# A decoder step on one core: block gate by 128-column groups, sample tables loaded earlier, a re-planned instruction order

## The chip, the cores and the metric

One Trainium2 chip, one core of it. The metric is the device time of one execution in microseconds (us), lower is better. The core has TensorE (PE in the profile), VectorE (DVE), ScalarE (ACT), GpSimd (POOL) and SyncE (SP, which here only issues DMAs); "q" behind an engine's name is its sequencer, which issues DMAs and loads registers in the engine's own order.

## The reference

One layer of a decoder, for 512 prompt positions and for 8 samples (one new token each, 4096 past positions in a paged cache). What matters for the change is the samples' attention:

```python
k_full = cache_k[page_table[:, :own_first]].reshape(Bd, n_full, MOBA_BLOCK, H, D)   # 16 blocks of 256
kmean = jnp.mean(k_full, axis=2)
gate = jnp.einsum('bhtd,bnhd->bhtn', qf, kmean)          # 8 heads x 16 blocks per sample
_, sel = lax.top_k(gate, topk)                            # 3 blocks for each head
...
kg = cache_k[pages, :, hidx]; vg = cache_v[pages, :, hidx]
s = jnp.einsum('bhtd,bhtkd->bhtk', qf, kg) * scale        # scores with the chosen blocks, ALiBi, softmax
```

Besides that: RMSNorm, one input projection 1024 x 3584 (for prompt and samples), a gated MLP over chunks, the prompt's attention, and one output projection 1024 x 1024 with a norm and the residual. All of it is fp32.

## The kernel before

The prompt's projections run on PE as seven chunks of 512 columns (order k, q, v, u, va, ga, gb), each of 4 tiles (`pj(c, t)`), a tile in four quarters of two matmuls. The trace shows a fp32 matmul as two records, so a quarter is 4 records `PA<-...`. The weights of a chunk (2 MB, `wbuf`, two buffers) are loaded by SP (step `wl(c)`, line 825), which first waits until the chunk two before is multiplied and a given batch of keys has landed. `spj(c)` (line 1044, `SB<-wbuf,hTs`) is the same chunk for the 8 samples: for each of 8 slices of the contraction, four matmuls of 128 columns, each into its own 32 output partitions. The output projection has two such chunks, 7 and 8 (`op`, line 1210, for the prompt; `fopa` and `fop`, line 1044, for the samples).

The samples are worked off one after the other, b = 0 to 7. For one b:

- POOL loads the 16 key blocks (`ld(b, n)`, line 931, 512 KB each) into 18 slots, at most 5 in flight; a slot comes free when the selected keys of the batch before are multiplied.
- DVE adds the two halves of each block (`ks(b, n)`, line 744) into one of 6 `ksum` tiles.
- PE adds over the positions (`gs`, line 1226): a matmul with a window of `win`, in which one column is ones, puts the block's sum on one row of bank `GB`. Four blocks go together, one to each 32 output partitions, 512 columns each.
- DVE's `ga(b)` multiplies `GB` by the query row `qb` (spread over all partitions), reduces to 4 values for each head, transposes, gathers with four copies into `g16`, and takes the top 3 (lines 1634 to 1658).
- DVE and POOL multiply the selected keys by q (`ex`, line 757); `pg` looks up pages and spreads the choice (`spread`, `selP`, lines 1664 to 1677); `bc`, `mt`, `mb` on PE and DVE (one bank `DC`) give scores, maximum and weights.
- The chosen value pages are fetched one at a time (`fetch(b, half, k, j)`, four DMAs each, line 728): two of three choices by SP, one by POOL. `pv0(b)` and `pv1(b)` on PE (line 1257) are the products with the values.

On SP, `qst` (line 833) stores the samples' queries to DRAM (`q_rows`) and `qb(b)` (line 841) spreads row b over the partitions. Behind `qb(0)` stands `load_sample_tables()`: 20 small DMAs (gain, two bias tables, the post-norm gain, x of the samples) that are first read by `spj` of chunk va.

Every engine works its list strictly in order. The lists come from `make_plan()`, a planner that runs ahead of the build: each step has a duration and what it needs, and at each point the step that can start first is taken (lanes break ties). The durations, the landing times of early loads, and the clocks at which engines start are numbers in the code.

## Time and profile before

| | |
|---|---|
| three runs | 415.79, 418.33, 429.66 us; median 418.33 |
| profiled execution | 421.29 us, of which the span of the profile is 419.5 us |
| PE busy | 390.1 us (93%) |
| POOL / DVE / ACT busy | 278.5 / 263.2 / 124.8 us |
| HBM traffic | 106.31 MB read, 4.29 MB written, 264 GB/s over the span |

The sum of a prediction is made against the 421.29 us of the profiled execution, and its difference is then taken from the median. Times in rows are microseconds from the span's start unless marked ns.

### The profile page before, as it was taken

Reading aid. Unit: us, or ns where it says so; the run is one execution under the profiler, and the core shown is the slowest. Engines: PE = TensorE matmul, PEld = TensorE weight load, DVE = VectorE, ACT = ScalarE, POOL = GpSimd, SP = SyncE. Lnnn points to the kernel's source line nnn. Section 1 sums busy time; section 2 is a strip of 40 time slices with the busy share of each in tenths; the row PEclk is TensorE's granted clock in tenths of the full one; section 3 lists DMA queues with packets and bytes.
Section 4 is the critical chain, followed back from the end, with each engine's and each line's share of the span. In section 5 each row is a group of like instructions: output and inputs, shape, how many; then the busy total and the mean of one; then the engine's idle time right before and its main releaser. Section 6 shows DMA issues by size and latency. Waiting matters only on the chain.

```text
span 419.5 us, 9227 instructions
## 1 busy us (share of the span) xinstructions
PE 390.1 (93%) x2790; PEld 183.9 (44%) x2790; DVE 263.2 (63%) x695; ACT 124.8 (30%) x279; POOL 278.5 (66%) x438
## 2 busy tenths in 40 slices
PE   7779996999999999999879999999898899989994
PEld 4534354334533454444534546345332454344451
DVE  1165495446944696459746996579656865694532
ACT  4211110000121436446634357546242012011020
POOL 6867764484668766757878777688768856675011
PEclk9999998999999999999989999999999899999998
DMA  8999389999599899977998199975999999925121
GB/s 274 368 395 375 123 268 381 336 287 284 198 352 361 189 354 345 333 185 270 292 316 241 34 367 344 308 155 155 337 367 328 318 380 397 198 63 108 67 99 53
DMA packets 78599, 111.22 MB, mean 265 GB/s; under 512 B 45744, under 2 KB 46896, under 8 KB 78552
## 3 DMA queue, kind: packets, MB, share of 16 engines
q0 software_dynamic: 22576, 71.45, 50.7%
q1 hardware_dynamic: 51992, 36.79, 31.3%
q10 hardware_dynamic: 3984, 2.41, 1.9%
q8 instruction: 22, 0.36, 0.4%
q14 instruction: 25, 0.20, 0.2%
HBM read 106.31 MB, written 4.29 MB: 264 GB/s over the span
## 4 chain that ended last, share of the span: by engine, by line
PE 18%; SPq 14%; DMA 7%; issue 7%; DVE 4%; POOL 3%; DVEq 1%; POOLq 0%; ACT 0%; ACTq 0%
PE PA L1210 14%; SPq L728 11%; DMA K<-in_cache_k,kidx 3%; DMA wbuf<-in_w_out 3%; DVE ksum L757 2%; DMA V<-in_cache_v 2%; POOL K L931 1%; SPq L724 1%; PE GB L1226 1%; PE SB L1044 1%; SPq L726 1%; PE SB L1196 1%; PE DC L1257 1%; POOL rstd L950 1%; POOL ksum L757 0%
## 5 line engine op out<-in xcount | busy, mean ns | idle before, releaser
L1101 PE MATMUL PA<-wbuf,hT 128*128 128x512 f32 x384 | 181.7, 611 | 1.2 <-DMA wbuf<-in_w_in 1.0
L931 POOL DMA_INDIRECT K<-in_cache_k,kidx x128 | 134.2, 1049 | 69.2 <-issue 36.4
L744 DVE TENSOR_TENSOR ksum<-K 128x512 f32<-128x512 f32 x128 | 86.2, 690 | 59.1 <-DMA K<-in_cache_k,kidx 52.6
L1101 PEld LDWEIGHTS PA<-wbuf,hT 128*128 128x128 f32 x384 | 69.2, 193 | 76.8 <-issue 74.2
L728 POOL DMA_DIRECT2D V<-in_cache_v x128 | 76.4, 599 | 16.8 <-issue 11.0
L1210 PE MATMUL PA<-wbuf,hT 128*128 128x512 f32 x128 | 59.2, 604 | 0.1
L757 DVE TENSOR_TENSOR ksum<-K,qb 128x128 f32<-128x128 f32 x128 | 41.1, 394 | 1.6 <-DVE selT L1658 1.3
L757 POOL TENSOR_TENSOR ksum<-K,qb 128x128 f32<-128x128 f32 x64 | 30.4, 507 | 12.2 <-DVE selT L1658 11.1
L1226 PE MATMUL GB<-ksum,win 128*32 128x512 f32 x256 | 34.1, 604 | 4.8 <-DVE ksum L744 4.8
L1210 PEld LDWEIGHTS PA<-wbuf,hT 128*128 128x128 f32 x128 | 22.9, 189 | 25.7 <-issue 25.2
L1101 PE MATMUL PA<-hT,wbuf 128*128 128x512 f32 x64 | 29.0, 599 | 0.0
L1690 DVE TENSOR_REDUCE sc<-ksum 128x48 f32<-128x3072 f32 x8 | 26.6, 3327 | 0.0
L1044 PE MATMUL SB<-wbuf,hTs 128*32 128x128 f32 x576 | 19.3, 289 | 6.3 <-DMA wbuf<-in_w_in 6.1
L1393 ACT ACTIVATE pr<-pr,smin 128x128 f32<-128x128 f32 (+3 forms) x32 | 17.7, 555 | 22.9 <-DVE smin L1580 22.8
L1359 ACT ACT_TABLE_LOAD x13 | 16.7, 1283 | 21.8 <-PE PA L1101 21.7
L947 POOL TENSOR_TENSOR rstd<-msum,nhalf 128x1 f32<-128x1 f32 x6 | 3.3, 550 | 27.6 <-DVE msum L1612 14.7
L1044 PEld LDWEIGHTS SB<-wbuf,hTs 128*32 128x32 f32 x576 | 16.4, 116 | 10.3 <-DMA wbuf<-in_w_in 5.0
L1402 ACT COPY pT<-SB 128x128 f32<-128x128 f32 (+3 forms) x32 | 12.6, 427 | 23.3 <-PE SB L1164 21.9
L1101 PEld LDWEIGHTS PA<-hT,wbuf 128*128 128x128 f32 x64 | 11.6, 190 | 13.7 <-issue 13.6
L1580 DVE CUSTOM_DVE_ANT_0 pr<-alibi,SB 128x128 f32<-128x128 f32 (+3 forms) x32 | 14.3, 484 | 4.4 <-PE SB L1155 4.3
L1257 PE MATMUL DC<-V,pex 128*32 128x64 f32 x768 | 13.9, 220 | 3.2 <-DMA V<-in_cache_v 3.2
L1305 ACT ACTIVATE junk<-PA 128x512 bf16<-128x512 f32 x8 | 4.8, 598 | 39.7 <-PE PA L1210 39.7
(226 smaller groups left out, 371.9 us busy)
## 6 DMA issues: line engine op xcount, KB each, us to landing
wbuf<-in_w_in SPq DMA_DIRECT2D x6, 2048.0 KB, 10.8
V<-in_cache_v SPq DMA_DIRECT2D x240, 32.0 KB
V<-in_cache_v POOLq DMA_DIRECT2D x128, 32.0 KB, 6.4
wbuf<-in_w_out SPq DMA_DIRECT2D x2, 2048.0 KB, 21.6
wbuf<-in_w_in SPq DMA_DIRECT2D x4, 512.0 KB, 10.3
K<-in_cache_k,kidx POOLq DMA_INDIRECT x128, 8.0
qb<-q_rows SPq DMA_DIRECT2D x8, 256.0 KB
v<-in_x_prompt ACTq DMA_DIRECT2D x2, 512.0 KB, 9.6
```

What stands on the lines that cost most here:

```text
L728: eng.dma_start(V[j * ROWS:(j + 1) * ROWS, x * TOP + k, :, :], v_pages[bass.ds(page, 1), :, :, HEAD[x] * HD:(HEAD[x] + 1) * HD] .rearrange ...
L744: eng.tensor_tensor(ksum[:, n % SUMS, :], K[:, at, 0, :], K[:, at, 1, :], ALU.add).then_inc(s_dsum, 1)
L757: last = eng.tensor_tensor(kq[:, x * TOP + k, :, :], K[:, bass.ds(n, 1), :, col:col + HD].rearrange("p a r d -> p (a r) d"), qb[:, col:col ...
L931: pool.indirect_dma_start(K[:, m % SLOTS, :, :].rearrange("p r w -> p (r w)"), None, k_rows, bass.IndirectOffsetOnAxis(ap=kidx[:, b, n:n + ...
L1044: last = pe.matmul(bank[32 * j:32 * j + 32, 0:P], src[:, kc, :], w[:, kc, j * P:(j + 1) * P], start=(kc == kcs[0]), stop=(kc == kcs[-1]), ...
L1101: last = pe.matmul(bank[:, :], lhs, rhs, start=(kc == 0), stop=(kc == KC - 1))
L1210: last = pe.matmul(bank[:, :], hT[:, kc, t * P:(t + 1) * P], wbuf[:, c % 2, kc, :], start=(kc == 0), stop=(kc == KC - 1))
L1226: last = pe.matmul(GB[32 * j:32 * j + 32, :], win[:, 31 - g:63 - g], ksum[:, (4 * g + j) % SUMS, :], start=(g == 0), stop=(g == G - 1), ti ...
L1257: last = pe.matmul(DC[32 * j:32 * j + 32, hh * HD:(hh + 1) * HD], pex[:, h, i, r:r + 1].broadcast_to([P, 32]), V[:, h * TOP + i, r, :], st ...
L1359: act.activation(dst, bank, fn, scale=sc_).then_inc(pa_free[n % 2], 1)
L1393: act.activation(pr[:, hh, 0:(i + 1) * P], pr[:, hh, 0:(i + 1) * P], ACT.Exp, bias=smin[:, hh:hh + 1], scale=-1.0, accum_out=ssum[:, 2 * p ...
L1690: dve.tensor_reduce(sc[:, :, :, :].rearrange("p h k r -> p (h k) r"), kq[:, :, :, :], AX.X, ALU.add).then_inc(s_scr, 1)
```

## The change

1. **Gate by 128-column groups.** The partition groups of the array now hold the four groups of 128 columns (two heads each) instead of four blocks: for each block there are four matmuls of 128 columns, group j reads `ksum[:, n, 128j:128j+128]`, and block n lands on row n of each partition group. The result is [4 x 32, 128] instead of [4 x 32, 512]. So `ga` multiplies 128 columns, reduces in four instructions of 32 partitions, and needs no gathering copies. `GB` holds two batches side by side (halves by b % 2), so `gs` of b no longer waits for `ga(b-1)` but for `ga(b-2)`. The blocks are summed in five lots, 4, 4, 4, 2, 2, instead of four of 4.
2. **A second spread of q.** `ga` needs q by groups of 128 columns: four more small DMAs in each `qb(b)`, ahead of the old one, into `qg` (the tile `qs`). `ga` waits on these (`s_qg`), and `multiply_selected` now waits for the old `qb` itself.
3. **Sample tables** are issued right behind the other small tables, ahead of everything in SP's list.
4. **Planner numbers**: a fetch on SP or ACT 4.2 instead of 3.1 us, values landed 4.0 instead of 2.5 us behind the last one, SP's start 28 instead of 20 us, `ga` 2.8 instead of 3.3, `qb(0)` 3.0 instead of 4.0, and the new `gs` steps. All engines' lists are made anew from them.

```diff
+BATCHES = [(0, 4), (4, 8), (8, 12), (12, 14), (14, 16)]
...
-            add("SP", "spread", ("qb", 0), 4.0, ("SP", ("qst",)))
+            add("SP", "spread", ("qb", 0), 3.0, ("SP", ("qst",)))
...
-                    add(eng, "fetch", ("fetch", b, hh, k, j), 2.5 if eng == "POOL" else 3.1, ("DVE", ("pg", b)), *free, *more)
+                    add(eng, "fetch", ("fetch", b, hh, k, j), 2.5 if eng == "POOL" else 4.2, ("DVE", ("pg", b)), *free, *more)
...
-        ends[eng, s] = clock[eng] + (0.0 if eng != "Q" else 2.5 if s[0] == "v" else 0.8)
+        ends[eng, s] = clock[eng] + (0.0 if eng != "Q" else 4.0 if s[0] == "v" else 0.8)
...
-PLAN_START = {"PE": 4.5, "ACT": 3.5, "DVE": 1.0, "POOL": 8.4, "SP": 20.0, "Q": 12.0}
+PLAN_START = {"PE": 4.5, "ACT": 3.5, "DVE": 1.0, "POOL": 8.4, "SP": 28.0, "Q": 12.0}
...
+            load_sample_tables()
             for s in PLAN["SP"]:
...
+                    sp.wait_ge(*((s_gate, b) if b else (s_snr, 1)))
+                    for j in range(G):
+                        sp.dma_start(qg[32 * j:32 * j + 32, :],
+                                     q_rows[b:b + 1, j * P:(j + 1) * P].broadcast_to([32, P])).then_inc(s_qg, 16)
                     sp.dma_start(qb[:, :], q_rows[b:b + 1, :].broadcast_to([P, W])).then_inc(s_qb, 16)
-                    if b == 0:
-                        load_sample_tables()
...
-                    if g == 0 and b >= 1:
-                        pe.wait_ge(s_gate, b)
-                    for j in range(4):
-                        last = pe.matmul(GB[32 * j:32 * j + 32, :], win[:, 31 - g:63 - g],
-                                         ksum[:, (4 * g + j) % SUMS, :], start=(g == 0), stop=(g == G - 1),
-                                         tile_position=(0, 32 * j))
+                    if g == 0 and b >= 2:
+                        pe.wait_ge(s_gate, b - 1)
+                    for n in range(lo, hi):
+                        for j in range(G):
+                            last = pe.matmul(GB[32 * j:32 * j + 32, (b % 2) * P:(b % 2 + 1) * P], win[:, 31 - n:63 - n],
+                                             ksum[:, n % SUMS, j * P:(j + 1) * P], start=(n == 0), stop=(n == NB - 1),
+                                             tile_position=(0, 32 * j))
...
-                    dve.wait_ge(s_qb, 16 * (b + 1))
-                    dve.tensor_tensor(sumq, GB[:, :], qb[:, :], ALU.mult).then_inc(s_gate, 1)
+                    dve.wait_ge(s_qg, 16 * G * (b + 1))
+                    dve.tensor_tensor(sumq, GB[:, (b % 2) * P:(b % 2 + 1) * P], qg, ALU.mult).then_inc(s_gate, 1)
...
-                    link(dve.tensor_reduce(g128[:, 0:H].rearrange("p (x j) -> p j x", x=2),
-                                           sumq.rearrange("p (j x d) -> p j x d", j=G, x=2), AX.X, ALU.add))
-                    link(dve.transpose(gT[:, :], g128[:, :]))
-                    for j in range(4):
-                        last = dve.tensor_copy(g16[:, :, j], gT[32 * j:32 * j + H, 0:G])
+                    for j in range(G):
+                        last = dve.tensor_reduce(g128[0:32, j:H:G], sumq[32 * j:32 * j + 32, :].rearrange("p (x d) -> p x d", x=2),
+                                                 AX.X, ALU.add)
                     link(last)
-                    gates = g16[:, :, :].rearrange("h g j -> h (g j)")
+                    link(dve.transpose(gT[0:32, :], g128[0:32, :]))
+                    gates = gT[0:H, 0:NB]
```

How SP's list stands near its beginning, before (from the last of the first small tables; `ks`, `yb` and `v` are stores of new rows):

```order
L789 DMA gain<-in_sgu_gain 128x512
L811 DMA out<-ks 8x128 x4
L807 DMA out<-yb 128x512
L833 DMA q_rows<-qs 8x128 x4
L841 DMA qb<-q_rows 128x512
L795 DMA gains<-in_sgu_gain 32x128
L796 DMA w<-in_sgu_w 32x1
L797 DMA b<-in_sgu_b 32x1
L798 DMA gposts<-in_g_post 32x2x128
L799 DMA xs<-in_x_sample 8x2x128
```

The last five rows come four times; then `out<-yb` twice and the weights of chunk 2. Now, from the last row of the tables' fourth round:

```order
L807 DMA xs<-in_x_sample 8x2x128
L820 DMA out<-ks 8x128 x4
L842 DMA q_rows<-qs 8x128 x4
L852 DMA qs<-q_rows 32x128 x4
L854 DMA qb<-q_rows 128x512
L816 DMA out<-yb 128x512 x3
L834 DMA wbuf<-in_w_in 128x8x512
```

So the 20 table DMAs moved from behind `qb` to ahead of `ks` and `q_rows`, and the weights of chunk 2 lost them from in front.

PE's list from the third lot of key sums of b = 0 (`GB`) to the first lot of b = 1, before (`spread` is `bc(0)`, `mx` is `mt(0)`, `SB<-wbuf,hTs` is `spj` of chunk 2):

```order
L1226 MATMUL GB<-ksum,win 32x512 x4
L1136 MATMUL SB<-ident,yb 128x128 x4
L1101 MATMUL PA<-wbuf,hT 128x512 x6
L1128 MATMUL SB<-pr,one 128x128 x4
L1101 MATMUL PA<-hT,wbuf 128x512 x2
L1136 MATMUL SB<-ident,yb 128x128 x4
L1101 MATMUL PA<-hT,wbuf 128x512 x6
L1233 MATMUL DC<-spread,one 128x24
L1101 MATMUL PA<-hT,wbuf 128x512 x2
L1044 MATMUL SB<-wbuf,hTs 32x128 x32
L1238 MATMUL DC<-ident,mx 8x128
L1101 MATMUL PA<-hT,wbuf 128x512 x2
```

and now (its first row is the last lot of b = 0):

```order
L1239 MATMUL GB<-ksum,win 32x128 x8
L1112 MATMUL PA<-wbuf,hT 128x512 x2
L1147 MATMUL SB<-ident,yb 128x128 x4
L1112 MATMUL PA<-wbuf,hT 128x512 x6
L1139 MATMUL SB<-pr,one 128x128 x4
L1112 MATMUL PA<-hT,wbuf 128x512 x2
L1147 MATMUL SB<-ident,yb 128x128 x4
L1112 MATMUL PA<-hT,wbuf 128x512 x4
L1246 MATMUL DC<-spread,one 128x24
L1112 MATMUL PA<-hT,wbuf 128x512 x4
L1251 MATMUL DC<-ident,mx 8x128
L1055 MATMUL SB<-wbuf,hTs 32x128 x32
```

The last key sums of b = 0 stand a quarter earlier, `bc(0)` a quarter earlier, and `mt(0)` now stands ahead of the samples' chunk 2.

PE's list near the end of the input projections, before (`SB<-wbuf,hTs` is `fopa(0)`, the first reader of the output weights; `SB<-ident,ya` turns the prompt's result):

```order
L1257 MATMUL DC<-V,pex 32x64 x24
L1101 MATMUL PA<-wbuf,hT 128x512 x4
L1251 MATMUL DC<-psm,one 32x2 x4
L1257 MATMUL DC<-V,pex 32x64 x24
L1101 MATMUL PA<-wbuf,hT 128x512 x2
L1196 MATMUL SB<-ident,ya 128x128 x4
L1044 MATMUL SB<-wbuf,hTs 32x128 x16
```

and now:

```order
L1270 MATMUL DC<-V,pex 32x64 x24
L1112 MATMUL PA<-wbuf,hT 128x512 x8
L1055 MATMUL SB<-wbuf,hTs 32x128 x16
L1112 MATMUL PA<-wbuf,hT 128x512 x6
L1264 MATMUL DC<-psm,one 32x2 x4
L1270 MATMUL DC<-V,pex 32x64 x24
L1239 MATMUL GB<-ksum,win 32x128 x16
L1207 MATMUL SB<-ident,ya 128x128 x4
```

The first reader of the output weights stands three quarters of a tile ahead of the end of the input projections, which it followed before; behind it come those quarters, the second value product of b = 5 and the first key sums of b = 7.

## Rows read from the trace of the kernel before

**Rows 1.** The page: busy time of each engine.
```profile
PE 390.1 (93%) x2790; PEld 183.9 (44%) x2790; DVE 263.2 (63%) x695; ACT 124.8 (30%) x279; POOL 278.5 (66%) x438
```

**Rows 2.** Who PE waited for: us in total, times, longest us.
```profile
PE SB L1044 <- DMA wbuf<-in_w_in: 6.1, 3, 3.5
PE GB L1226 <- DVE ksum L744: 4.8, 4, 1.7
PE DC L1257 <- DMA V<-in_cache_v: 3.2, 2, 2.5
PE DC L1055 <- DVE sc L1715: 2.1, 1, 2.1
PE DC L1251 <- issue: 2.0, 1, 2.0
```

**Rows 3.** SP's queue in order of time: start us, us, what.
```profile
17.98 13.18 SPq L789 DMA_DIRECT2D sgub<-in_sgu_b  x1
31.20 3.84 SPq L789 DMA_DIRECT2D gain<-in_sgu_gain  x1
35.09 1.38 SPq L811 DMA_DIRECT2D out<-ks  x4
...
36.92 1.35 SPq L833 DMA_DIRECT2D q_rows<-qs  x4
46.13 0.34 SPq L841 DMA_DIRECT2D qb<-q_rows  x1
...
56.46 0.67 SPq L799 DMA_DIRECT2D xs<-in_x_sample  x1
...
58.21 0.39 SPq L825 DMA_DIRECT2D wbuf<-in_w_in  x1
```

**Rows 4.** PE in order of time, first two batches; idle before it in brackets.
```profile
31.42 1.95 PE L1044 MATMUL SB<-wbuf,hTs 128*32 128x128 f32 x64
...
43.01 5.42 PE L1101 MATMUL PA<-wbuf,hT 128*128 128x512 f32 x12
...
69.08 3.43 PE L1044 MATMUL SB<-wbuf,hTs 128*32 128x128 f32 x64 [3.48 <-DMA wbuf<-in_w_in]
...
74.36 1.06 PE L1226 MATMUL GB<-ksum,win 128*32 128x512 f32 x8
```

**Rows 5.** DVE in order of time, around the gate of b = 0.
```profile
34.04 0.28 DVE L1548 TENSOR_TENSOR mix<-qs,ks 128x128 f32<-128x128 f32 x1
...
49.49 0.69 DVE L1634 TENSOR_TENSOR ksum<-GB,qb 128x512 f32<-128x512 f32 x1 [3.24 <-PE GB L1226]
...
51.18 0.89 DVE L1642 COPY g<-gT 8x4 f32<-8x4 f32 x4
...
60.00 0.17 DVE L1673 TENSOR_TENSOR spread<-ident,vals 8x24 f32<-8x24 f32 x1
...
66.38 0.20 DVE L1704 TENSOR_REDUCE mx<-sc 128x8 f32<-128x48 f32 x1
```

**Rows 6.** Line 728, value fetches: from issue to landing.
```profile
DMA to landing us min/median/max: 2.0/6.4/9.7
```

**Rows 7.** 45 to 50 us: busy PE, PEld, DVE, ACT, POOL; clock, DMA, GB/s.
```profile
45.00:50.00 5.00, 5.00 (x21) 1.97 (x21) 1.25 (x3) 0.69 (x1) 3.83 (x17) 1.00 0.20 63
```

**Rows 8.** PE in order of time, from 215 us on.
```profile
215.04 0.24 PE L1055 MATMUL DC<-msum,fold 128*32 128x1 f32 x8 [2.12 <-DVE sc L1715]
215.21 7.11 PE L1101 MATMUL PA<-wbuf,hT 128*128 128x512 f32 x12
...
301.51 1.07 PE L1226 MATMUL GB<-ksum,win 128*32 128x512 f32 x8 [1.71 <-DVE ksum L744]
...
326.71 0.88 PE L1257 MATMUL DC<-V,pex 128*32 128x64 f32 x48 [2.50 <-DMA V<-in_cache_v]
```

**Rows 9.** DVE: the last key block of b = 6.
```profile
317.05 0.69 DVE L744 TENSOR_TENSOR ksum<-K 128x512 f32<-128x512 f32 x1 [2.27 <-DMA K<-in_cache_k,kidx]
```

**Rows 10.** Line 825, weight loads: from issue to landing.
```profile
DMA to landing us min/median/max: 9.2/11.0/21.6
```

More of the change, by code:

```diff
@@ L53, in v_queue, with batch_of @@
     return ("SP", "POOL", "ACT")[k]
+def batch_of(n):
+    return [lo <= n < hi for lo, hi in BATCHES].index(True)
 def make_plan():
@@ L248, in make_plan @@
             if n >= SUMS:
-                deps.append(("PE", ("gs", b, (n - SUMS) // 4)))
+                deps.append(("PE", ("gs", b, batch_of(n - SUMS))))
             add("DVE", "gate", ("ks", b, n), 0.75, *deps)
@@ L252, in make_plan @@
             add("POOL", "load", ("const",), 8.5)
-        for g in range(G):
-            late = [("DVE", ("ks", b, n)) for n in range(4 * g, 4 * g + 4)]
-            add("PE", "gate", ("gs", b, g), 1.0, *late, *([("DVE", ("ga", b - 1))] if b else []))
+        for g, (lo, hi) in enumerate(BATCHES):
+            late = [("DVE", ("ks", b, n)) for n in range(lo, hi)]
+            add("PE", "gate", ("gs", b, g), 0.25 * (hi - lo), *late, *([("DVE", ("ga", b - 2))] if b >= 2 else []))
         used = [("Q", ("v", b - 2, hh, k)) for hh in range(2) for k in range(TOP)] if b >= 2 else []
-        add("DVE", "gate", ("ga", b), 3.3, ("PE", ("gs", b, G - 1)), ("SP", ("qb", b)), *used)
+        add("DVE", "gate", ("ga", b), 2.8, ("PE", ("gs", b, len(BATCHES) - 1)), ("SP", ("qb", b)), *used)
         parts = [("ex", b, i) for i in range(PARTS)]
@@ L506, in hymba_kernel @@
         iota16 = sb("iota16", [H, NB])
-        g16 = sb("g16", [H, G, 4])
         top8 = sb("top8", [H, 8])
@@ L602, in hymba_kernel @@
         s_qb = sem("q_row_spread")
+        s_qg = sem("q_row_spread_by_groups")
         s_yas = sem("yas_ready")
@@ L624, in hymba_kernel @@
         kq = ksum[:, :, :].rearrange("p s (x r d) -> p (s x) r d", x=4, r=2)
-        sumq = ksum[:, 0, :]
+        sumq = ksum[:, 0, 0:P]
+        qg = qs[:, :]
         xres = [qT[:, 0:2, :], qT[:, 2:4, :], kT[:, 0:2, :], kT[:, 2:4, :]]
@@ L741, in sum_rows @@
             if n >= SUMS:
-                eng.wait_ge(s_gs, G * b + (n - SUMS) // 4 + 1)
+                eng.wait_ge(s_gs, len(BATCHES) * b + batch_of(n - SUMS) + 1)
             at = (NB * b + n) % SLOTS
@@ L746, in multiply_selected @@
         def multiply_selected(eng, b, which, name):
+            eng.wait_ge(s_qb, 16 * (b + 1))
             rows = {}
@@ L1219, in _ @@
                     b, g = s[1], s[2]
-                    pe.wait_ge(s_dsum, NB * b + 4 * g + 4)
+                    lo, hi = BATCHES[g]
+                    pe.wait_ge(s_dsum, NB * b + hi)
                     if (b, g) == (0, 0):
                         pe.wait_ge(s_ones, 1)
-                    if g == 0 and b >= 1:
-                        pe.wait_ge(s_gate, b)
-                    for j in range(4):
-                        last = pe.matmul(GB[32 * j:32 * j + 32, :], win[:, 31 - g:63 - g],
-                                         ksum[:, (4 * g + j) % SUMS, :], start=(g == 0), stop=(g == G - 1),
-                                         tile_position=(0, 32 * j))
+                    if g == 0 and b >= 2:
[5 more added lines that the diff above has]
+                                             tile_position=(0, 32 * j))
                     last.then_inc(s_gs, 1)
@@ L1631, in _ @@
                     b = s[1]
-                    dve.wait_ge(s_gs, G * (b + 1))
-                    dve.wait_ge(s_qb, 16 * (b + 1))
-                    dve.tensor_tensor(sumq, GB[:, :], qb[:, :], ALU.mult).then_inc(s_gate, 1)
+                    dve.wait_ge(s_gs, len(BATCHES) * (b + 1))
+                    dve.wait_ge(s_qg, 16 * G * (b + 1))
+                    dve.tensor_tensor(sumq, GB[:, (b % 2) * P:(b % 2 + 1) * P], qg, ALU.mult).then_inc(s_gate, 1)
                     dve.wait_ge(s_gate, b + 1)
```

## The prediction

> **What bounds the kernel now.** I read the page first: PE is busy for 390.1 of 419.5 us [rows 1], so no other engine bounds the whole, and everything but PE's work and PE's waits is cover. What a change can win is the 29.4 us of idle, and of these only what lies between the start and the end. So the second view is the list of whom PE waited for [rows 2]: 6.1 us for input weights in three waits, 4.8 for key blocks, 3.2 for values, 2.1 for a score step on DVE that held bank `DC`, 2.0 for another value landing; 18.2 us in all. A wait also costs clock: behind the 3.48 us wait at 69.08 the 64 records of `spj` took 3.43 us, against 1.95 for the same 64 at 31.42 [rows 4], so 1.5 us; behind the wait at 215.04, 12 records took 7.11 us [rows 8] against 5.42 [rows 4], so 1.7 us. At 326.71 there is another wait of that size [rows 8], and I count 1.7 us there too. The third view is SP's queue [rows 3]: it tells why the first long wait is there.
>
> **Sample tables (SP).** Before, the 20 table DMAs run from 46.47 (the end of `qb(0)`) to 57.13 us: 10.7 us, 0.53 us each [rows 3]. The weights of chunk 2 are issued behind them, at 58.21, and PE stands until 69.08 [rows 3, 4]. In the change nothing but `qb(0)` and three stores is in front. The weights then wait for their own condition, PE's end of chunk 0: PE runs 12 records from 43.01 [rows 4], and with what the new list puts up to the end of chunk 0 that comes at 55 to 56 us. So they are issued some 3 us earlier, at a time at which the DMA engines are at 0.20 of their capacity [rows 7]. A load takes 9.2 to 21.6 us, median 11.0 [rows 10]; on quiet engines I take the low end, and they land at about 65, ahead of `spj`. The wait and its clock go.
>
> But every DMA that moves forward is moved past something. The tables are now ahead of `out<-ks` and of the store of q. The store, issued at 36.92 before, is issued after 35.04 + 10.7 + 1.4 = 47.1 and is through at 48.5. Before, SP waited from 38.27 to 46.13 for that store to land [rows 3], under key loads; now it falls where the engines are quiet [rows 7], and I take the shortest landing of a small DMA in the trace, 2.0 us [rows 6]: 50.5. Then four small spreads, 0.53 each, 52.6, and again 2.0: q is there for `ga(0)` at 54.6 us. Before, `ga(0)` began at 49.49, and what it waited for was PE, not q [rows 5]. So q takes the place of the weights as what is late: by about 5 us.
>
> How much of this reaches PE: `ga` gets shorter (next part) by 1.0 us, so from its start to `spread` it is 60.17 - 49.49 - 1.0 = 9.7 us, and from there to the end of `mx` 66.58 - 60.17 = 6.4, less 0.7 for the 512-column step of chunk q that stood between and now stands behind: 5.7 [rows 5]. `mt(0)` can start at q + 15.5. Behind it PE has 4.0 us (`mt`, `spj`, one quarter, and the semaphore between) to the first key sums of b = 1: q + 19.6, which is 74.2 us with q at 54.6. Before, it was 74.36 [rows 4]. Without the late q, PE would be there at 70.2: from 43.01 on 9 quarters of 1.8, 1.0 of key sums, 1.9 of small steps and `bc` to 62.3, two quarters, then 4.0 and some tenths. **Term 1: -4.2 for the weights, +4.0 for q, -0.2 us.** Ends: with q at 52 it is -2.7; with landings of 6.4 us instead of 2.0 [rows 6] only for the spreads it is +4.2.
>
> **Gate by groups.** PE: before, a lot of four blocks is 8 records in 1.0 to 1.1 us [rows 4]. After it is 32 records of 128 columns, in four partition groups. The same form is in the trace: `spj`, 64 records in 1.95 us [rows 4], so 32 in 0.98. The columns streamed are the same and so is the time. The extra lot of each batch splits a run of matmuls once more; a new run costs about 0.15 us (5.42 for 12 against 3 x 1.75), so 8 x 0.15 = **term 2: +1.2 us**. The bank is shared by two batches, which removes a wait of PE that is in no row; nothing.
>
> On this there is a rule of the Trainium skill that speaks against the change (page "TensorE: Matmul & The Clock Gate", section "Back-to-back issue gap"): in a stream of weight loads and matmuls the sustained spacing is about 81 ns at 128 columns and 131 ns at 512. By it, four short ones would cost 2.5 times one long one. The 8 x 16 x 2 = 256 records of the gate at some 0.13 us each are 34 us, and would become 84. The trace has 30 ns for a record of 128 columns in partition groups, so I don't follow the rule here.
>
> DVE: one multiplication of 0.69 becomes 0.28, the price of 128 columns [rows 5]; the reduction, as long, becomes four of 128 columns, which I price at the 0.28 of the multiplication; four copies, 0.89, go. 0.69 + 0.69 + 0.89 = 2.3 against 0.28 + 1.1 = 1.4: `ga` is 0.9 to 1.0 us shorter. DVE is busy 63% and bounds nothing; the gain lies on the chain from `ga` to the freeing of key slots, and shortens each batch's cycle of loads. Against it, SP issues four more spreads (2.1 us) between `ex` and the fetches of values, of which some 1 us falls into its wait for `selP`. For values the two cancel; for keys 1 us is left.
>
> **New order.** This is the part that can win, and it can't be priced step by step. What goes: the wait of 2.1 us at 215.04 with its 1.7 us of clock, because the step that needed bank `DC` there (`ra`, the samples' norm) now stands far behind. **Term 3: -3.8 us.** What may go: 4.8 for keys, 3.2 + 1.7 for values, 2.0 at the second product of b = 6 [rows 2, 8]. The list gives `bc` and the second value product of several batches 5 to 8 us of PE work more room. But it moves the key sums of b = 5 and 6 forward by 4 to 5 us of PE work, and there the keys were late already: PE waited 1.71 at 301.51, and the last block of b = 6 came 2.27 us late for DVE too [rows 8, 9]. The cycle of key loads is 1 to 1.5 us faster now, not 4 to 5. The first value product of b = 5 also stands nearer to its gate, by some 3 us, where it waited 2.50 [rows 8]. And `fopa(0)` is moved ahead of 5.4 us of projection, 0.9 of value product and 1.0 of key sums: the output weights have that much less time. I take it that in this part new waits are as large as those that go, 10.5 us against 10.5: **term 4: 0**, with ends -10 and +8.
>
> **Sum**: -0.2 + 1.2 - 3.8 + 0 = -2.8 us; 421.29 becomes 418.5. The median of the runs is 2.96 below the profiled one, so I forecast 418.33 - 2.8 = **415.5 us**, no difference that this kernel's measurement can tell (about 2%, 8.4 us).
>
> **Rivals.**
> - *All late waits vanish.* The new fetch durations fit the trace, and no wait replaces the old ones: -2.8 - 10.5 = -13.3 on the median, 405 us. For it: the fetches on SP really were longer than the plan had them. Against it: the key cycle [rows 9].
> - *The tables stall SP* (slower). The engines are full at 35 us; a small table was held 13.18 us in SP's queue at 17.98, and the next 3.84 [rows 3]. If the 20 DMAs take 1.0 us each instead of 0.53, q comes at 64 and PE at 83.6 instead of 74.2: +9.4, 425 us. It turns slower from q at 57.4 on. Against it: the nine DMAs issued from 35.09 to 38.27 were not held [rows 3].
> - *The output weights are late* (slower). If they take 21.6 us instead of 11.0 [rows 10] with the reader 7.3 us earlier, PE stands about 8 us more at `fopa(0)`, and there is nothing else in its list: 423.5 us. From a landing of some 3 us over the median on, it costs more than the other terms win.
> - *Short matmuls are not free.* Were each priced at even double its columns, the gate's 34 us would double: 452 us. The rows of `spj` exclude it nearly. The skill's spacing would give 466, and its chance is in here.
>
> **How the numbers follow.** Forecast 0.50; vanishing waits 0.20; stalled tables 0.12; late output weights 0.13; short matmuls 0.02; the rest, 0.03, is near no change. Faster by over 2% (under 410.0) needs most of the late waits gone: 0.20. Slower by over 2% (over 426.7) needs a rival at its upper end or two of them: 0.13. Within 2%: 0.67. The range reaches to the vanishing waits and to the stalled tables: 405 to 425.
>
> **What would show it.** Right: no wait at `spj` of chunk 2, waits of PE of about 2 us each at `bc(0)` and `mt(0)`, `ga(0)` starting at 54 to 55 us behind a DMA of `qs`, first key sums of b = 1 at 74 to 75; the wait at `ra` gone; 32 gate records in about 1 us; waits for keys near b = 6 still there. Wrong: `ga(0)` before 51 or after 58, a gate lot of 1.5 us or more, or the sum of PE's waits in the last third under 3 or over 15 us.

## The result: 4.4% slower

| | before | after |
| --- | --- | --- |
| median of 4 runs, us | 419.98 (415.79 to 429.66) | 438.96 (433.53 to 441.15) |
| ratio, 95% interval | 1 | 1.0443 (1.0274 to 1.0613) |
| profiled execution, us | 421.29 | 439.66 |
| its span, us | 419.5 | 437.7 |
| its mean granted clock of TensorE | 0.985 | 0.972 |

The changed kernel is 19 us slower, outside the range of 405 to 425. All ratios in this section leave disturbed runs out, so a ratio can differ a little from that of two medians.

The busy line of the page after the change, beside [rows 1]:

```profile
PE 398.2 (91%) x3558; PEld 206.2 (47%) x3558; DVE 258.3 (59%) x687; ACT 123.5 (28%) x278; POOL 278.3 (64%) x438
```

PE is busy 8.1 us longer and idle 39.5 us instead of 29.4; the two make the 18.2 us of the span. Only 3.6 of the 8.1 lie in the gate's records (37.7 us against 34.1). The granted clock tells of more. It has two levels, full and half, and its mean of 0.985 before and 0.972 after means about 13 and 24 us at the half level: 6 us more of full clock are lost. Before, it fell at three waits of PE (69.08, 215.04 and 326.71) and in the tail; after, at five (28.01, 157.07, 217.73, 245.17 and 347.05) and in the tail. So more waits, and clock behind them.

Who PE waited for after the change (us in total, times, longest), beside [rows 2]:

```profile
PE GB L1239 <- DVE ksum L751: 7.0, 6, 2.5
PE SB L1055 <- DMA wbuf<-in_w_in: 5.4, 2, 3.8
PE DC L1251 <- DVE mx L1716: 4.8, 3, 2.2
PE SB L1055 <- DMA wbuf<-in_w_out: 4.2, 1, 4.2
PE DC L1246 <- DVE spread L1685: 2.3, 1, 2.3
PE SB L1199 <- DVE ya L1582: 2.2, 1, 2.2
```

No wait is large; there are many, and most are in new places. Only values (1.6 us against 3.2) and input weights (5.4 against 6.1) are waited for less. **The first 80 us went as worked out.** SP's queue after the change, beside [rows 3]:

```profile
30.52 4.35 SPq L797 DMA_DIRECT2D gain<-in_sgu_gain  x1
34.91 0.43 SPq L803 DMA_DIRECT2D gains<-in_sgu_gain  x1
...
45.16 0.68 SPq L807 DMA_DIRECT2D xs<-in_x_sample  x1
45.88 1.48 SPq L820 DMA_DIRECT2D out<-ks  x4
47.41 1.31 SPq L842 DMA_DIRECT2D q_rows<-qs  x4
50.88 1.70 SPq L852 DMA_DIRECT2D qs<-q_rows  x4
52.62 0.42 SPq L854 DMA_DIRECT2D qb<-q_rows  x1
...
57.07 0.39 SPq L834 DMA_DIRECT2D wbuf<-in_w_in  x1
```

The tables take 10.9 us in the queue and aren't held; q follows. PE in order of time, first beside [rows 4], then at the places where it falls back:

```profile
65.78 0.37 PE L1246 MATMUL DC<-spread,one 8*128 8x24 f32 x2 [2.26 <-DVE spread L1685]
...
71.53 0.27 PE L1251 MATMUL DC<-ident,mx 128*8 128x128 f32 x1 [1.75 <-DVE mx L1716]
71.73 1.95 PE L1055 MATMUL SB<-wbuf,hTs 128*32 128x128 f32 x64
...
75.52 1.08 PE L1239 MATMUL GB<-ksum,win 128*32 128x128 f32 x32
...
157.07 3.18 PE L1055 MATMUL SB<-wbuf,hTs 128*32 128x128 f32 x64 [3.80 <-DMA wbuf<-in_w_in]
...
217.73 0.27 PE L1251 MATMUL DC<-ident,mx 128*8 128x128 f32 x1 [2.16 <-DVE mx L1716]
217.84 5.29 PE L1112 MATMUL PA<-wbuf,hT 128*128 128x512 f32 x8
...
245.17 0.63 PE L1199 MATMUL SB<-ident,oT 128*128 128x128 f32 x4 [2.20 <-DVE ya L1582]
...
347.05 1.93 PE L1055 MATMUL SB<-wbuf,hTs 128*32 128x128 f32 x32 [4.19 <-DMA wbuf<-in_w_out]
```

The weights of chunk 2 are in time (71.73, no bracket), and a lot of 32 gate records takes 1.08 us. Matching the projection's records of both traces (they are the same in number and order) gives how far the changed kernel is behind; single tiles scatter, since steps between them moved: 1.2 us at the start of the third tile of chunk 1, 2.5 at that of the second of chunk 3, 8.6 at the last quarter of this tile, 5 to 7 in the next, about 12 to 14 in the last two tiles of chunk 5, 13 to 19 in chunk 6, 20 to 22 in the first half of the output, 18.2 at the end. The 157.07 row is the first large step: the weights of chunk 4 are late, and the 64 records behind the wait take 3.18 us instead of 1.95. They were issued at 143.18, 2 us earlier than before (145.22), but PE got them 13.9 us later; before it was 9.2. Behind 217.73, 8 records take 5.29 us, where 12 at full clock take 5.42 [rows 4].

DVE in order of time in b = 4, and POOL's next key load:

```profile
235.78 0.29 DVE L1647 TENSOR_TENSOR ksum<-GB,qs 128x128 f32<-128x128 f32 x1 [1.62 <-PE GB L1239]
...
242.12 1.86 DVE L1540 SCALAR_TENSOR_TENSOR vn<-vn,rstd,gain 128x128 f32<-128x128 f32 x4 [3.48 <-POOL rstd L961]
...
244.95 2.01 DVE L765 TENSOR_TENSOR ksum<-K,qb 128x128 f32<-128x128 f32 x8
...
252.55 0.89 DVE L765 TENSOR_TENSOR ksum<-K,qb 128x128 f32<-128x128 f32 x4
```

```profile
253.72 1.11 POOL L942 DMA_INDIRECT K<-in_cache_k,kidx  x1 [6.48 <-DVE ksum L765]
```

The key slots of b = 4 come free when DVE's last `ksum<-K,qb` is done. The new list puts projection and attention steps between the four parts, so from the gate's multiply to the next key load it is 17.9 us; before it was 11.9 (229.09 to 241.04).

### The profile page after: what moved, and what is told of

It is laid out like the page before. It is cut to its first block, busy times and chain, and to the rows that moved or that the text cites. A ratio compares the mean times of both kernels' runs of the same rounds, so it can differ in the third digit from the quotient of the medians.

```text
span 437.7 us, 10796 instructions
## 1 busy us (share of the span) xinstructions
PE 398.2 (91%) x3558; PEld 206.2 (47%) x3558; DVE 258.3 (59%) x687; ACT 123.5 (28%) x278; POOL 278.3 (64%) x438
## 4 chain that ended last, share of the span: by engine, by line
PE 19%; DMA 14%; issue 10%; POOL 10%; POOLq 1%; DVE 0%; DVEq 0%; ACT 0%; ACTq 0%; SPq 0%
PE PA L1221 13%; DMA K<-in_cache_k,kidx 9%; DMA wbuf<-in_w_out 5%; POOL K L942 4%; POOL V L735 2%; POOL ksum L765 2%; PE PA L1112 2%; PE SB L1055 1%; POOL rstd L961 1%; PE GB L1239 1%; PE SB L1207 1%; PE DC L1270 1%; POOLq L731 1%; POOL rstd L960 0%; POOLq L733 0%
## 5 line engine op out<-in xcount | busy, mean ns | idle before, releaser
L1112 PE MATMUL PA<-wbuf,hT 128*128 128x512 f32 x384 | 184.7, 618 | 1.6 <-DMA wbuf<-in_w_in 1.4
L1221 PE MATMUL PA<-wbuf,hT 128*128 128x512 f32 x128 | 59.5, 604 | 0.3 <-issue 0.3
L1239 PE MATMUL GB<-ksum,win 128*32 128x128 f32 x1024 | 37.7, 281 | 7.8 <-DVE ksum L751 7.0
L1239 PEld LDWEIGHTS GB<-ksum,win 128*32 128x32 f32 x1024 | 26.5, 111 | 35.0 <-DVE ksum L751 18.5
L765 DVE TENSOR_TENSOR ksum<-K,qb 128x128 f32<-128x128 f32 x128 | 40.1, 382 | 1.8 <-DVE selT L1670 1.3
L1112 PE MATMUL PA<-hT,wbuf 128*128 128x512 f32 x64 | 29.4, 602 | 0.0
L1647 DVE TENSOR_TENSOR ksum<-GB,qs 128x128 f32<-128x128 f32 x8 | 2.3, 292 | 23.1 <-PE GB L1239 13.7
## 6 DMA issues: line engine op xcount, KB each, us to landing
wbuf<-in_w_in SPq DMA_DIRECT2D x6, 2048.0 KB, 11.2
```

The source lines that it names most:

```text
L765: last = eng.tensor_tensor(kq[:, x * TOP + k, :, :], K[:, bass.ds(n, 1), :, col:col + HD].rearrange("p a r d -> p (a r) d"), qb[:, col:col ...
L1112: last = pe.matmul(bank[:, :], lhs, rhs, start=(kc == 0), stop=(kc == KC - 1))
L1221: last = pe.matmul(bank[:, :], hT[:, kc, t * P:(t + 1) * P], wbuf[:, c % 2, kc, :], start=(kc == 0), stop=(kc == KC - 1))
L1239: last = pe.matmul(GB[32 * j:32 * j + 32, (b % 2) * P:(b % 2 + 1) * P], win[:, 31 - n:63 - n], ksum[:, n % SUMS, j * P:(j + 1) * P], start ...
```

## The experiments

Eighteen kernels, in the order in which they ran. "Old gate" and "old order" are those of the kernel before. The medians stand beside those of the kernel before on the same chip.

**1. The change in four pieces.** g1: the new gate with four lots instead of five, tables in their old place, old numbers; every list is that of before. t1: before, tables early. n1: before, the three planner numbers. a1: the changed kernel, the three numbers back. The pieces:

```diff
-                    if b == 0: load_sample_tables()    (behind qb(0))
+            load_sample_tables()                      (ahead of SP's list)   t1
-  2.5 if eng == "POOL" else 3.1    2.5 if s[0] == "v"    "SP": 20.0
+  2.5 if eng == "POOL" else 4.2    4.0 if s[0] == "v"    "SP": 28.0          n1, and back in a1
```

> The gate by 128-column groups and the second spread of q alone: four lots of four blocks, the sample tables at their old place, every planner number as before, so that every engine's list of steps is word for word the one of before. Theory 'order' (the 18 us are lost by the new lists): 417 to 422 us, no difference from before beyond 2 or 3 us; PE's gate work 34 to 35 us. Rival 'gate' (the short matmuls and the four more DMAs are what costs): 425 to 430 us. Rival 'late q' (the tables in front of q): like 'order' here.

> The kernel before with only the 20 table DMAs moved ahead of SP's list; all lists of steps as before. Theory 'order': 416 to 422 us; the wait of 3.5 us at the samples' chunk 2 goes, the gate of b = 0 starts at 54 to 55 us instead of 49.5. Rival 'late q' (the delay of the first gate, some 5 us, is carried to the end by the key loads): 424 to 428 us. Rival 'gate': as before.

> The kernel before with only three planner numbers changed: a fetch on SP or ACT 4.2 instead of 3.1, values landed after 4.0 instead of 2.5, SP's start 28 instead of 20. Instructions are the same, their order is not. Theory 'order': most of the loss is here, 427 to 436 us, with DVE's selected-key products broken up by steps of the prompt or weights and sums waiting in PE's list. Rivals 'gate' and 'late q': 416 to 422 us.

> The changed kernel with the same three planner numbers taken back (gate by groups in five lots and early tables stay, with the lists that the planner makes of them). Theory 'order': 418 to 426 us, most of the 18 us comes back. Rivals 'gate' and 'late q': 434 to 440 us, as the changed kernel.

| kernel | median, before | ratio (95%) |
| --- | --- | --- |
| g1 | 432.18, 421.24 | 1.0269 (1.016 to 1.0379) |
| t1 | 423.49, 421.24 | 1.0092 (1.0047 to 1.0137) |
| n1 | 441.88, 421.24 | 1.0493 (1.0391 to 1.0594) |
| a1 | 432.53, 421.24 | 1.0269 (1.0181 to 1.0357) |

No time fell into the range of its own theory: g1 came out above even the range of the rival, n1 above that of 'order', t1 and a1 between two ranges. The order alone does not hold: the gate costs 2.7% where not one step has moved. The numbers alone cost 4.9% on the kernel before, yet taking them out of the changed kernel gives back 6.4 us of 19. The pieces don't add, since each trips over waits of its own. n1 has two of them late, on PE:

```profile
328.95 1.93 PE L1044 MATMUL SB<-wbuf,hTs 128*32 128x128 f32 x32 [5.25 <-DMA wbuf<-in_w_out]
...
367.29 0.29 PE L1251 MATMUL DC<-psm,one 128*32 128x2 f32 x8 [10.54 <-issue]
```

In g1 the waits of PE for key sums are 11.2 us and for input weights 8.8 (4.8 and 6.1 in [rows 2]), while PE's busy time rises by 1.8 only:

```profile
PE GB L1240 <- DVE ksum L751: 11.2, 7, 3.1
PE SB L1056 <- DMA wbuf<-in_w_in: 8.8, 3, 6.3
```

**2. What of the new gate costs.** s1: before, with the four small spreads of q added on SP's queue, read by nobody. g2: g1 with one DMA for the four spreads. p1: before, each gate record of 512 columns cut into four of 128. b1: before, tables right ahead of the weights of chunk 3.

```diff
+ for j in range(G):                                                         s1
+     sp.dma_start(qs[32 * j:32 * j + 32, :], q_rows[b:b + 1, j * P:(j + 1) * P].broadcast_to([32, P]))
- (the same four, into qg)                                                   g2
+ sp.dma_start(qg, q_rows[b:b + 1, :].rearrange("o (j d) -> j o d", j=G).broadcast_to([G, 32, P]))
- ksum[:, (4 * g + j) % SUMS, :]                                             p1
+ for x in range(4): ... ksum[:, (4 * g + j) % SUMS, x * P:(x + 1) * P]
+ if c == 3: load_sample_tables()    (ahead of wl(3))                        b1
```

> The kernel before, with the four small spreads of q of each b added on SP's queue ahead of the large one (into a tile that nobody reads); gate, lists and tables as before. The gate change in the old order cost 11 us (1.027). Theory 'queue': most of that is what the four spreads hold up on SP's queue (the weights of chunk 2, about 4 us, then the fetches of values): 425 to 431 us. Theory 'gate form' (128-column records, the sums by groups): the spreads are hidden, 418 to 423 us, and the 11 us stay with the kernels that have the new gate.

> The new gate in the old order, with one DMA that spreads q by groups where there were four (so one more issue on SP per b than before instead of four more). Theory 'queue': three quarters of the loss go, 420 to 424 us. Theory 'gate form': still 430 to 434 us.

> The kernel before, its 256 gate records of 512 columns cut into 1024 of 128 columns with the same sums, the same places in the bank and the same multiply behind them; nothing else moves. Theory 'gate form': the short records (or their fourfold weight loads) cost time that the busy column doesn't show, 426 to 432 us. Theory 'queue': 418 to 422 us, and lots of 16 records at a mean near 0.28 us each in the overlapped count, as in the changed kernel.

> The kernel before, with the twenty loads of the samples' tables issued right ahead of the weights of chunk 3 instead of behind the first spread of q; their first reader is at 162 us. Both theories of the gate are silent on it; it measures the term of the weights of chunk 2 by itself: the wait of 4.2 us at chunk 2's first samples' matmul goes, without the late q of the kernel with the early tables. 414 to 418 us if the 4 us stay gained, 418 to 421 if the next wait (keys, values) gives them back.

| kernel | median, before | ratio (95%) |
| --- | --- | --- |
| s1 | 429.81, 421.84 | 1.0276 (1.0094 to 1.0458) |
| g2 | 427.95, 421.84 | 1.014 by the medians, no interval |
| p1 | 425.27, 421.84 | 1.0168 (0.9988 to 1.0349) |
| b1 | 427.08, 421.84 | 1.0238 (1.0041 to 1.0436) |

Only s1 came out in a stated range, that of 'queue'; g2 and p1 fell between two ranges. Spreads that nobody reads cost as much as the whole new gate with its spreads, but s1 holds up SP's queue too, so it doesn't separate issue from transfer. p1 decides nothing: its interval takes in no change. b1 missed its own forecast by 6 us or more, and its trace says why. SP's queue and PE there:

```profile
92.47 1.39 SPq L795 DMA_DIRECT2D gains<-in_sgu_gain  x1
...
103.27 0.68 SPq L799 DMA_DIRECT2D xs<-in_x_sample  x1
104.05 0.41 SPq L827 DMA_DIRECT2D wbuf<-in_w_in  x1
```

```profile
116.18 3.51 PE L1044 MATMUL SB<-wbuf,hTs 128*32 128x128 f32 x64 [8.56 <-DMA wbuf<-in_w_in]
```

Up to chunk 2 it was 3.9 us ahead of the kernel before, the term of the weights that I had computed. Then the same 11 us of tables made the weights of chunk 3 late.

**3. Places, and single faults of the new order.** b2: tables right behind the weights of chunk 3. g3: the same with the new gate and one spread. d1: the changed kernel, DVE's four parts of each b put next to each other. f1: the changed kernel, `fopa(0)` back behind the last projection tile.

```diff
+ if c == 3: load_sample_tables()    (behind wl(3))                          b2, g3
+ line = PLAN["DVE"]; at = line.index(("ex", b, 0))                          d1
+ line[at + 1:] = parts + [s for s in line[at + 1:] if s not in parts]
+ PLAN["PE"], PLAN["ACT"]: ("fopa", 0) to behind ("yt", 0, 0), ("pj", 6, 3)  f1
```

> The kernel before, with the twenty table loads issued right behind the weights of chunk 3, where SP's queue stood idle for 9 us in the trace of before (from 96 to 104.7 us), and not ahead of them. With the tables ahead of those weights the 4 to 5 us of chunk 2's weights were gained and a wait of 8.6 us at chunk 3's took them back twice. If the weights were the whole of it, both waits are gone here: 414 to 418 us, below the kernel before by 1%. Rival: the value fetches of b=1 behind the tables come 8 us late and a wait at pv0(1) or at the weights of chunk 4 takes the place: 419 to 424 us.

> The new gate in the old order with one DMA for the spread by groups, and the tables behind the weights of chunk 3. With the queue cleared, what stays is the gate form by itself: theory 'queue' 415 to 420 us (the gate costs nothing of its own), theory 'gate form' 421 to 427 us. Both expect no wait at chunk 2's weights.

> The changed kernel, with DVE's four parts of the score products of each b put next to each other (in b=4 five steps of the projection and of the attention stood between the first and the last, in b=5, 6 and 7 up to two). Theory 'order of DVE': in b=4 the stretch from the gate's multiply to the next key load falls from 17.9 to about 12 us, the keys of b=5 and all that follows come 3 to 6 us earlier: 433 to 436 us. Rival: what is put behind them is itself late for PE, and the time stays at 438 to 441 us.

> The changed kernel, with fopa(0), the first reader of the output weights, put back on PE and ACT to behind the last projection tile and the first transposes, where it stood before. Theory 'output weights': the wait of 4.2 us and the 7 us at half the clock behind it go, 432 to 435 us. Rival: the next reader of the same weights, the first output tile, stands 5 to 10 us on and waits in its place or something later ends the path: 437 to 441 us.

| kernel | median, before | ratio (95%) |
| --- | --- | --- |
| b2 | 420.24, 423.12 | 1.0047 (1.0006 to 1.0088) |
| g3 | 431.57, 423.12 | 1.0283 (1.0209 to 1.0358) |
| d1 | 436.88, 423.12 | 1.04 (1.0291 to 1.051) |
| f1 | 439.15, 423.12 | 1.0418 (1.0272 to 1.0565) |

b2 and f1 came out in the range of the rival, d1 between two ranges, g3 above both. d1 cut the stretch in b = 4 from 17.9 to 13.4 us, and 2 us came out, which the runs can't tell from nothing. f1 removed the wait of 4.19 us and gained nothing; PE stands a few us on instead:

```profile
349.90 0.21 PE L1267 MATMUL DC<-psm,one 128*32 128x2 f32 x5 [2.08 <-issue]
...
352.96 1.30 PE L1242 MATMUL GB<-ksum,win 128*32 128x128 f32 x20 [1.97 <-DVE ksum L754]
```

b2 was built on SP's idle time from 96 to 104.7 us, and is level with the kernel before within 1% (its interval lies just above 1). g3 was no clean test. The tables fill that idle time to the last, so that a delay of 2.4 us at the weights of chunk 3 goes on down the queue. SP's queue in b2, then in g3, and PE in g3:

```profile
91.97 0.54 SPq L825 DMA_DIRECT2D wbuf<-in_w_in  x1
103.40 0.43 SPq L816 DMA_DIRECT2D out<-v  x1
...
141.13 0.46 SPq L825 DMA_DIRECT2D wbuf<-in_w_in  x1
```

```profile
94.34 0.55 SPq L833 DMA_DIRECT2D wbuf<-in_w_in  x1
107.14 0.44 SPq L824 DMA_DIRECT2D out<-v  x1
...
149.92 0.47 SPq L833 DMA_DIRECT2D wbuf<-in_w_in  x1
```

```profile
168.87 3.64 PE L1054 MATMUL SB<-wbuf,hTs 128*32 128x128 f32 x64 [16.70 <-DMA wbuf<-in_w_in]
```

In this profiled execution 2.4 us at 92 have become 8.8 at 141, and at chunk 4's weights 16.7 us of PE.

**4. The queue relieved.** Eleven table loads instead of twenty: three of the five tables for all four groups at once. m1: before with it. m2: new gate, old order, one spread, with it. m3: the changed kernel, one spread, with it. m4: m1, and each gather of result rows as one DMA instead of four. m5: m3 with the old three numbers. m6: m1 with the short records of p1.

```diff
- sp.dma_start(gains[rows, :], sgu_gain[:, j, :].broadcast_to([32, P]))      (four times; w00 and b00 too)
+ sp.dma_start(gains[:, :], sgu_gain.rearrange("l g c -> g l c").broadcast_to([G, 32, P]))
- for j in range(G): sp.dma_start(obs[32 * j + b:32 * j + b + 1, :], osb[32 * j:32 * j + 1, b % 2, :])
+ sp.dma_start(obs[b:P:32, :], osb[0:P:32, b % 2, :])                        m4
```

> The kernel before, with eleven loads for the samples' tables where there were twenty (three of the five tables loaded for all four groups at once), in their old place. Theory 'queue' (SP's queue is what bounds the stretch from 46 to 160 us): SP is free 4 us earlier, the weights of chunk 2 are in time and nothing behind them is pushed: 413 to 418 us. Rival: the time that the issue takes goes with the bytes and rows, not with the count, and nothing changes: 420 to 423 us.

> The new gate in the old order, with one spread by groups and eleven table loads, so that SP's queue issues 8 DMAs fewer up to the weights of chunk 2 than before. Theory 'queue': the whole loss of the gate goes, 415 to 421 us. Theory 'gate form': 425 to 431 us, with the waits of PE for sums and for values as in the earlier run.

> The changed kernel with one spread by groups and eleven table loads; lists as in the changed kernel. The q of the first sample is then on its way 4 to 5 us earlier, and each b has three issues fewer on SP. Theory 'queue alone': 420 to 428 us. Theory 'order' (the loss sits in the lists that the three numbers give): 432 to 437 us.

> As the kernel before with eleven table loads, and each gather of a sample's result rows (four DMAs of 0.85 us of SP per sample) as one DMA over four partitions. Theory 'queue': the weights of chunks 4 to 6 and the value fetches behind each gather start 2.5 us earlier, 411 to 417 us, 0 to 3 us below the run without it. Rival: SP has slack behind the gathers, and the time is that of the run without it.

> The changed kernel with one spread by groups, eleven table loads, and the three numbers of the planner back at 3.1, 2.5 and 20. Theory 'numbers': nearly all of the 8 us go, 424 to 428 us. Theory 'rest of the plan' (tables ahead of q, five lots): 430 to 434 us.

> The old gate with its 256 records of 512 columns cut into 1024 of 128 columns, and eleven table loads; the old spread, the old multiply, the old lists. Theory 'records' (four times the weight loads and records cost by themselves): 423 to 427 us, as the new gate with the relief (425.0). Theory 'path around' (second spread, its wait, the longer chain behind the sums): 418 to 421 us, as the old gate with the relief (419.7).

| kernel | median, before | ratio (95%) |
| --- | --- | --- |
| m1 | 419.7, 422.15 | 0.9933 (0.9888 to 0.9978) |
| m4 | 418.66, 422.15 | 0.9967 (0.9914 to 1.002) |
| m6 | 421.9, 425.2 | 0.9988 (0.9925 to 1.0051) |
| m2 | 424.98, 422.15 | 1.0058 (1.0002 to 1.0114) |
| m5 | 430.1, 425.2 | 1.021 (1.0095 to 1.0325) |
| m3 | 433.39, 422.15 | 1.0297 (1.0226 to 1.0368) |

m2 came out at the lower end of 'gate form', m3 in the range of 'order', m4 in that of the rival, m5 in that of 'rest of the plan'; m1 and m6 fell between two ranges. This is the ladder that settles which pieces cost. From m1 to m2, the new gate without the crowded queue, it is 1.25%, 5.3 us, and the intervals don't meet. From m2 to m3, the new lists, 2.4%, 10 us, and again they don't meet. From m3 to the changed kernel, the twelve DMAs more in the first batch and three more in each later one, 1.4%, 6 us, with intervals that overlap. m1 itself is 0.7% faster than the kernel before: fewer loads, and nothing moved past anything. Its trace has no wait for chunk 2's weights, but those of m4 and m6, which have the same eleven loads and issue these weights at 55.2 and 55.4 us (m1 at 56.57), still wait 2.37 and 3.12 us for them. So this wait depends on the landing as much as on the queue, and that its end is m1's gain is not shown. m1 is the one version here whose interval lies below 1; m4's gathers add nothing that shows. The step from m1 to m2 can be cut once more, at m6: 0.55% for the short records and 0.7% for the rest (second spread, its wait, the new multiply), and in both halves the intervals overlap. Of the 2.4% of the lists the numbers are at most the smaller part (m5 to m3, 0.9%, intervals overlap); the others are the early tables, the five lots and the changed costs.

**What the second spread does.** For every trace I took the key loads of b = 2 to 7: from the first key load behind the gate's multiply of the batch before (two blocks are loaded ahead of it) to the end of the batch's last key sum on DVE, summed over the six batches, and beside it from the gate's multiply to the next key load.

| kernel | loads to last sum, us | multiply to load, b = 1 to 6, us |
| --- | --- | --- |
| before | 188.5 | 63.6 |
| m1 / m4 | 188.6 / 187.4 | 64.4 / 64.3 |
| m6 (short records, old spread) | 186.6 | 64.9 |
| s1 (old gate, spreads added) | 199.6 | 63.9 |
| m2 (new gate, one spread) | 197.1 | 62.9 |
| g1 / m3 | 196.3 / 199.8 | 62.9 / 62.4 |
| after | 199.8 | 68.6 |

Of the eighteen kernels and the two at the start, ten have a second spread and no stall of 8 us or more at weights: 195.6 to 203.9. Eight have none and no such stall: 186.6 to 192.6. They don't overlap, whatever the gate's form. (b1 has 195.2, with 38.3 in the batch in which PE stood 8.6 us; g3 has 212.9, with 50.6 in that of the 16.7 us.) So with the second spread the keys of a batch take 1.2 us longer (g2 less before, over six), 1.4 (m2 less m1) or 1.8 (s1 less before); the profiled executions of m2 and s1 were 1 and 5 us longer than their medians, so 1.2 is the safest of the three. The chain from the gate's multiply to the choice is 0.7 to 0.9 us shorter, but little of that reaches the keys: the second column falls by 1.5 us over six batches from m1 to m2, and by 0.7 from before to g1. In b = 4 to 6 of m2 POOL begins its share of the products 2.9 to 5.3 us behind the choice, so the choice isn't what it waits for. From m1 to m2 the keys lose 8.5 us in all and the time is 5.3 longer. This stretch accounts for the gate alone: n1 has one of the short ones and is the slowest version. The transfers show where the keys lose. Windows of 1 us behind the spread of b = 3, first m1, then m2 (busy PE, PEld, DVE, ACT, POOL; granted clock, DMA share, GB/s):

```profile
149.00:150.00 1.00, 1.00 (x3) 0.38 (x2) 1.00 (x1) 0.00 (x0) 0.69 (x2) 1.00 1.05 389
150.00:151.00 1.00, 0.96 (x4) 0.29 (x2) 1.00 (x1) 0.00 (x0) 0.69 (x2) 1.00 0.98 256
151.00:152.00 1.00, 0.00 (x0) 0.00 (x0) 1.00 (x4) 0.23 (x1) 0.81 (x1) 1.00 0.88 266
```

```profile
150.00:151.00 1.00, 1.00 (x4) 0.34 (x2) 1.00 (x1) 0.00 (x0) 0.89 (x1) 1.00 1.00 367
151.00:152.00 1.00, 0.73 (x3) 0.29 (x2) 1.00 (x2) 0.00 (x0) 0.69 (x2) 1.00 0.47 147
152.00:153.00 1.00, 0.00 (x0) 0.00 (x0) 1.00 (x5) 0.74 (x3) 0.69 (x2) 1.00 0.57 182
153.00:154.00 1.00, 0.53 (x20) 0.53 (x24) 0.93 (x2) 0.98 (x3) 0.54 (x1) 1.00 0.82 309
```

A large spread issued at 146.73 in m1 is followed by two windows at two thirds of the 400 GB/s around them: 144 + 134 missing is 0.7 us of key traffic. In m2, with both spreads issued at 147.22 and 147.90, three windows miss 253 + 218 + 91, 1.4 us. In s1, behind its spreads of b = 3, four windows (279, 300, 198, 197) miss 626, 1.6 us. Batch 4 shows the same, in the 5 us from the first issue of a spread, m1 and then m2:

```profile
192.02:197.02 5.00, 5.00 (x16) 2.01 (x18) 4.86 (x9) 2.46 (x9) 3.84 (x4) 1.00 0.71 209
```

```profile
193.22:198.22 5.00, 4.99 (x69) 2.65 (x70) 4.86 (x9) 3.20 (x12) 3.83 (x4) 1.00 0.59 122
```

That is 1.04 MB against 0.61, 1.1 us of traffic at 400 GB/s. That these dips are the spreads is read from their time; no run took the spread itself away, and none added it to m1 alone.

On the one DMA that replaces four there is a rule in the Trainium skill (page "DMA: Bandwidth & Descriptors", section "Rules for kernel authors"): a transfer whose outermost dimension counts fewer than 16 is confined to that many of the engines, and the outermost dimension of this one is 4. The DMA share of 0.47 and 0.57 in m2 agrees with it. That s1, whose spreads have 32 rows outermost, loses as much speaks against it as the whole cause: there the share stays at 0.82 to 0.94 in the four windows, so the engines are busy and move less. No run here separates the two.

## Why the prediction was wrong

The sum was -2.8 us and the change cost 19. Two of its terms failed: term 2, by 4 us and more, with 6 more for its DMAs on the crowded queue (m3 to the changed kernel), and term 4, by 10. Terms 1 and 3 didn't.

**Term 1, weights and q (-0.2 us): right in mechanism, and near in size, where it was read.** `ga(0)` was forecast at 54.6 and began at 55.8, behind q; the waits at `bc(0)` and `mt(0)` are 2.26 and 1.75 us (about 2 each); the first key sums of b = 1 are at 75.52 (74.2), 1.2 us behind the kernel before, where a lag of 1.4 had arisen at the first key sums of b = 0 already (a wait of 2.50 us at 28.01, against 1.15, and the lot behind it at half the clock). Behind chunk 2's weights b1, b2 and m1 are 3.3 to 4.1 us ahead of the kernel before (4.2). But t1, the tables alone, is 1.009: some 4 us are lost by the end, though its profiled execution was 1.2 us faster than that of before. The profile didn't show that loss.

**Term 2, gate by groups (+1.2 us): the first failed step.** The lot of 32 records took 1.08 us (0.98), the chain behind it is 0.7 to 0.9 us shorter (0.9 to 1.0), and the records by themselves cost 0.55% (m1 to m6, overlapping intervals). All that was right or near, and the term still is 11 us with the queue as it was (g1) and 5 with it relieved (m1 to m2). What I had mis-sized is the sentence on SP: "four more spreads (2.1 us) between `ex` and the fetches of values, of which some 1 us falls into its wait ... for values the two cancel; for keys 1 us is left". I priced their issue on SP, against an idle time of SP further on. I didn't price their transfer, though it falls where the DMA engines are full of keys, and I didn't ask which wait on SP's queue has slack (in g1 chunk 2's weights are issued at 60.22 instead of 58.21, and PE waits 6.29 us for them instead of 3.48). And I let the whole shorter chain reach the keys. The keys lose 1.2 us or more per batch and win some 0.2. How much of the 5 us is the transfer and how much the records stays open (m6).

**Term 3, the wait at `ra` (-3.8 us): right and worth nothing.** The wait at 215.04 [rows 8] is gone. 2.7 us further on PE waits 2.16 us for `mx`, and the clock falls behind it just as it did.

**Term 4, new order (0, from -10 to +8): the second failed step, and the largest miss.** m2 to m3 puts it at 10 us, outside its ends. I set it to nothing by taking new waits to be as large as those that go, and no row stood behind that; the waits that may go also add up to 11.7 us (4.8 + 3.2 + 1.7 + 2.0), not 10.5, which would put the low end of the range at 404. I set waits against one another on PE's list. I never looked at DVE's list, where the parts of b = 4 were pulled apart, nor at what the weights of chunk 4 would land among (157.07). And I gave the new waits no more clock than the 1.7 us of the one that may go: of the six of over 2 us in the rows after the change, five took another 1 to 2 us each (28.01 among them); that of 2.26 at 65.78 took none.

**The rivals.** "All late waits vanish" did not come: PE's waits in the last third are 9.2 us, where they were 8.0. "The output weights are late" came true as a wait (4.19 us and half the clock behind it, forecast 8), but it was no cause: f1 took it away and won nothing. "The tables stall SP" did not happen (0.43 to 0.90 us each). "Short matmuls are not free" is excluded at its price (m6); 32 records in 1.08 us are 34 ns each, so the spacing of 81 ns that the Trainium skill gives (page "TensorE: Matmul & The Clock Gate", section "Back-to-back issue gap") does not hold for records in four partition groups. None of the four held the case that came: the new DMAs slow down the keys, and the new lists cost 10 us in the middle. The signs were badly chosen. All those for being right showed, within some 1 us, and of those for being wrong only one did, by the way: the first gate lot, at 28.01, took 1.93 us, because it ran at half the clock. Waits in the last third under 3 or over 15 us did not show; most of the loss lay between 150 and 300 us, where I had set no sign.

**What stays open:** which part of the lists costs most of the 10 us. d1 and f1 each undid one fault and won 2 us and nothing, n1 has other faults than the changed kernel. That speaks for little slack at many places rather than one step; it is not shown. Why t1 is slower than its trace is open too, and so is why chunk 4's weights took 13.9 us.

## What to carry to other kernels

Price a new DMA three times: its issue on the queue, what is queued behind it there, and its transfer beside whatever the DMA engines carry at that moment; if they are full, even 64 KB to all partitions per batch may cost more than the compute step that it saves, as it seems to here. A queue near its limit has no cheap places: before a step is moved on it, find the next condition with a deadline behind the new place (here the next weights), and prefer fewer DMAs to moved ones. In a kernel ordered by hand or by a planner, a removed wait is worth nothing until the next late resource is known, and a new order costs until shown otherwise.

## What the runs showed of the hardware

A 128-partition spread of one 2 KB row moves 256 KB, and behind that of b = 3 in m1 the core's traffic fell from about 400 to 260 GB/s for 2 us. Behind a further 64 KB of the same kind, in m2, twice as much was missing (1.4 us of traffic instead of 0.7). A load of 128 small rows for four groups in one DMA took 0.52 to 0.73 us of SP's queue, against four DMAs of 0.42 to 0.43 us each in the kernel before. A load of 2 MB of weights was there for PE 9.2 us behind its issue or 13.9 us, by what else was being loaded (chunk 4, before and after). The kernel before ran from 415.3 to 431.1 us over all measurements, and its median from 419.98 to 425.2 us; so ratios against runs on the same chip at the same time are needed for anything under 2%.
